# A decoder block on one core: loads and gathers moved across stage joins, row refills ahead of x, conditioning shared with TensorE

## The chip, the cores and the metric

The kernel runs on one core of one Trainium2 chip. The metric is the device time of one execution in microseconds (us); lower is better. The time before is the median of three runs. The profile is of one further execution, taken by the hardware profiler.

## The reference, cut to what matters

One layer of a decoder block over 2048 tokens of width 1024, all in float32. The conditioning vector c gives six vectors; a delta-rule head group and a dilated attention head group share one projection; a mixture of 32 experts follows.

```python
def reference(x, c, w_ada, b_ada, norm_mix, w_in, w_conv, ..., norm_final):
    for l in range(DEPTH):
        mod = c @ w_ada[l] + b_ada[l]                                  # 1024 x 6144
        sh_a, sc_a, gt_a, sh_f, sc_f, gt_f = jnp.split(mod[:, None, :], 6, axis=-1)
        h = rmsnorm(x, norm_mix[l]) * (1.0 + sc_a) + sh_a
        x = x + gt_a * hybrid_mixer(h, w_in[l], w_conv[l], ..., w_out[l], rel_bias[l])
        h = rmsnorm(x, norm_ffn[l]) * (1.0 + sc_f) + sh_f
        x = x + gt_f * hierarchical_moe(h, w_router_group[l], w_router_expert[l], w_gate[l], w_up[l], w_down[l])
    return rmsnorm(x, norm_final)

# hybrid_mixer: p = h @ w_in; first 1536 columns -> causal convolution of 4 taps, SiLU -> q, k, v of 4 heads
#   gated delta rule in chunks: a unit lower triangular solve per chunk, then a state carried over the chunks
#   attention of 8 heads in three dilated windows, merged by their log-sum-exp, rms norm
#   y = concat(delta rule part * silu(z), attention part) @ w_out
# hierarchical_moe: best of 4 groups, best 2 of its 8 experts, blocks of tokens per expert:
#   hid = silu(xb @ w_gate[e]) * (xb @ w_up[e]); ys = hid @ w_down[e]; out.at[tok].add(ys * gate)
```

## The kernel before, in words

`block_kernel` runs seven stages one after the other, with a barrier of all engines between them: `condition_and_project`, `project_channels`, `deltanet`, `attention`, `mix_and_route`, `experts`, `finish`. Each stage opens a `Room`, which takes its on-chip tiles and semaphores. Before the stage's work SyncE raises every semaphore of the stage that has a credit, one instruction each (L159); other engines enter the stage at once, but each wait includes the credit. At the end a room clears its semaphores and meets at the barrier (L138). The order of work on each engine is written out by hand in every stage; SyncE issues nearly all DMAs, strictly in program order, and stands at each `wait_ge` before them. Tokens are in 16 tiles of 128 (NT = 16, P = 128), D = 1024 = KD x 128.

**condition_and_project.** The six vectors are computed in 12 blocks of 512 columns (BANK), the first FIRST = 4 before all else, since they are shift and scale. The weights `w_ada` of a block come in two halves of 1 MB through NW = 3 buffers (`load_half`). VectorE multiplies each half's four slices with its scalars of c and adds them (`weigh`, L363 and L365: 4 instructions a half); then TensorE sums over the partitions with a matrix of ones (`over_partitions`, L285) and VectorE adds the bias (`take_mod`, L376). When all four are there, VectorE makes the gain (L399) and the first tiles of h, TensorE turns them (`turn`, L292) and multiplies with the token weights `wt` (L309), 4 MB in four DMAs, all of which it waits for. In the loop over the 16 tiles one more half per tile is weighed.

**project_channels.** TensorE computes 20 channels of 128 rows over 2048 tokens: 4 groups of 512 tokens each, 8 products a group (`group`, L644), weights `w_chan` of 0.5 MB a channel through two buffers (`load_w`, L509). ScalarE copies each group out of PSUM (`take_group`, L729); group n+2 waits for the copy of group n. At the start ScalarE computes decay values first (L759 to L763), after three small DMAs. The last channels run beside the solve of small 32 x 32 blocks on VectorE; SyncE stores the channels to DRAM (`store_cv`) and the solved blocks (`store_blocks`).

**deltanet.** A loop over 16 chunks. Per chunk SyncE loads `nt`, four pairs of small diagonal blocks into zeroed tiles `dz` and `dzt` (`load_solve`), `kc`, `vb`, `kg`, `qg`, `aqk` (`load_chain`), `z`, and, for the first eight chunks, 1 MB of q/k channels for the attention. TensorE's products (`heads`, L1050) and VectorE's masks and differences (L1164, L1170, L1174) alternate in one chain per chunk; L1136 is ScalarE's copy of a chunk's solution. VectorE begins with two operations on `nrm` (L1155, L1157) that need a square root of ScalarE. GpSimd zeroes `dz` and `dzt` at the start.

**mix_and_route** (the output stage). Per tile t and, in the code, its buffer b and count q: VectorE merges the three attention parts (`differences`, L1699 to L1701; `weigh`, L1705 to L1714; `normed`, L1718 and L1719), TensorE turns y (`turn_y`), multiplies with `w_out` (`out`, L1621, 32 records), turns h of an earlier tile (`turn_h`) and computes its router logits (L1615). VectorE adds the result to x (`add_out`, L1722 and L1723), normalizes (`router_in`, L1735 to L1737), and routes pairs of tiles (`choose` and `place` in alternate slots), whose lists GpSimd scatters to DRAM (L1581). In slot t VectorE does: `add_out(t-1)`, `weigh(t+2)`, `choose` or `place`, `router_in(t-1)`, `normed(t+2)`, `differences(t+3)`. TensorE in step t: `turn_y(t+1)`, `turn_h(t-2)`, `out(t)`, logits of t-2, ranks. ScalarE in slot t ends with the exponential of t+3 (L1886), then the logits copy (L1908), for which TensorE's next `turn_h` waits. SyncE's loop decides when rows come:

```python
with sp.Fori(0, NT // 2 - 2) as i:
    for b in range(2):
        load_x(2 * i + (2 + b), b, i + 1)     # waits for x2_out and h_ready of two tiles before
        load_y(2 * i + (4 + b), b, i + 2)     # waits for yt_done: y of two tiles before is turned
```

`load_y` loads 256 KB of y (L1545) and 792 KB of attention rows into `mo` (L1547). After the last x the stage loads the gate/up weights of the first NWB = 4 experts, 2 MB each, into `big`. After the last tile the places are computed on VectorE, GpSimd gathers the lists, and VectorE writes `slot_tok` (L1872) and `slot_gate` (L1873).

**experts.** Blocks of two half blocks of 64 rows. GpSimd gathers 128 rows of h by index (`gather`, L2060), TensorE turns them (L2094), ScalarE copies them (L2151), TensorE multiplies the upper half with `wgu` and the lower with a copy `wgu2` (L2108, L2109), which ScalarE makes (`copy_gate_up`, L2159); VectorE copies the w_down block (`copy_down`, L2195). At the start SyncE loads the four w_down blocks (L2030), 1 MB each, and only then reports them and the gate/up blocks as loaded.

## Time and profile before

| | |
|---|---|
| median of three runs | 2518.68 us (2518.53 to 2520.19) |
| the profiled execution | 2507.53 us, span 2505.4 us |
| mean granted TensorE clock | 0.949 |
| TensorE products | 2206.2 us busy (88% of the span) |
| VectorE | 1126.5 us (45%) |
| ScalarE | 922.0 us (37%) |
| GpSimd | 382.8 us (15%) |
| read from and written to memory | 296.84 and 124.85 MB |

A stage can be told by its lines: `condition_and_project` from 0 to 296 us, `project_channels` to 971, `deltanet` to about 1160, `attention` to 1515, `mix_and_route` to 1897, `experts` to about 2440, `finish` to the end. In the timeline one row is an instruction, or several alike on one engine merged (x8): start, duration, engine, line, operation, output<-inputs, shapes, and in brackets how long the engine had been idle before and what released it. A product in float32 leaves two records on TensorE. SPq rows are SyncE's issues of DMAs, not their transfers. The granted clock is 1.00 in the rows of a stretch that TensorE began cold, too; at 1.2 GHz a record of 512 columns takes about twice the time that it takes at 2.4 GHz.

### The profile page before, as it was taken

How to read it: one execution, taken by the hardware profiler on the slowest of the kernel's cores; microseconds unless marked ns; L12 is line 12 of the kernel's file. 1: busy time of each engine (PE TensorE's matmuls, PEld its weight loads, DVE VectorE, ACT ScalarE, POOL GpSimd, SP SyncE). 2: the span in 40 equal slices, each digit the busy share in tenths (PEclk: the TensorE clock that was granted, in tenths of full speed). 3: DMA queues.
4: the chain of work that ended last, by engine and by line, in shares of the span. 5: the costliest groups of instructions: out<-in, count | busy, mean ns of one | idle time of the engine just before them, and what ended most of it. 6: DMA issues, size and time to landing. Idle time of an engine off the chain costs nothing. (4 is left out here: it accounts for less than half of the span.)

```text
span 2505.4 us, 33260 instructions
## 1 busy us (share of the span) xinstructions
PE 2206.2 (88%) x9964; PEld 1242.9 (50%) x9965; DVE 1126.5 (45%) x2294; ACT 922.0 (37%) x2136; POOL 382.8 (15%) x320
## 2 busy tenths in 40 slices
PE   3999899999988897897999998878885998999990
PEld 2666544444444445896777774444552333333330
DVE  5444222232233752555888775656652222222223
ACT  1333111111233311224778774323323443444433
POOL 0000000000011101344333110010012222222220
PEclk9999999999999998998999999988887999999995
DMA  8444102211255544985223324343354988989747
GB/s 341 147 153 147 50 34 90 104 59 50 99 173 178 182 178 131 311 261 200 89 92 105 102 89 162 127 119 99 121 210 148 306 261 284 328 249 312 218 80 287
DMA packets 178320, 418.13 MB, mean 167 GB/s; under 512 B 41192, under 2 KB 81000, under 8 KB 162744
## 3 DMA queue, kind: packets, MB, share of 16 engines
q1 hardware_dynamic: 155944, 346.59, 39.6%
q0 software_dynamic: 13472, 45.26, 7.8%
q10 hardware_dynamic: 8816, 25.18, 2.9%
q8 instruction: 46, 0.75, 0.1%
q14 instruction: 42, 0.34, 0.0%
HBM read 296.84 MB, written 124.85 MB: 168 GB/s over the span
## 5 line engine op out<-in xcount | busy, mean ns | idle before, releaser
L644 PE MATMUL ps<-big,pc_w 128*128 128x512 f32 x1280 | 558.0, 597 | 10.6 <-DMA pc_w<-in_w_chan 10.6
L644 PEld LDWEIGHTS ps<-big,pc_w 128*128 128x128 f32 x1280 | 243.9, 192 | 312.3 <-issue 300.9
L2108 PE MATMUL ps<-big,ex_xt 128*64 x672 | 302.2, 603 | 2.1 <-ACT ex_xt L2151 2.1
L2109 PE MATMUL ps<-ex_wgu,ex_xt 128*64 128x512 f32 x672 | 302.2, 603 | 0.0
L1621 PE MATMUL ps<-w_out,mo_yt 128*128 128x512 f32 x512 | 235.5, 619 | 0.0
L309 PE MATMUL ps<-cp_wt,big 128*128 128x344 f32 x768 | 225.4, 454 | 0.0
L2159 ACT COPY ex_wgu<-big 128x4096 f32 x43 | 155.1, 3607 | 84.7 <-SPq L2025 51.9
L309 PEld LDWEIGHTS ps<-cp_wt,big 128*128 128x128 f32 x768 | 145.8, 191 | 76.9 <-issue 4.0
L1363 PE MATMUL ps<-at_v,at_pt 128*128 128x128 f32 (+1 forms) x1200 | 182.8, 290 | 0.0
L1429 ACT ACTIVATE at_p<-at_p,at_low 128x256 f32<-128x256 f32 (+1 forms) x384 | 174.0, 456 | 19.1 <-DVE at_low L1392 18.8
L2108 PEld LDWEIGHTS ps<-big,ex_xt 128*64 128x64 f32 x672 | 89.7, 139 | 181.1 <-issue 181.1
L1363 PEld LDWEIGHTS ps<-at_v,at_pt 128*128 128x128 f32 x1200 | 149.1, 191 | 46.1 <-issue 36.4
L1621 PEld LDWEIGHTS ps<-w_out,mo_yt 128*128 128x128 f32 x512 | 101.6, 202 | 121.3 <-issue 121.0
L2120 PE MATMUL ps<-ex_wd,ex_hidt 128*64 x336 | 153.2, 598 | 2.7 <-DVE mod L2185 1.5
L2121 PE MATMUL ps<-ex_wd,ex_hidt 128*64 128x512 f32 x336 | 153.2, 598 | 0.0
L1390 DVE SCALAR_TENSOR_TENSOR at_p<-ps,bias 128x512 f32<-128x512 f32 (+1 forms) x192 | 109.3, 569 | 68.0 <-PE ps L1338 67.9
L1338 PE MATMUL ps<-at_kb,at_qb 64*128 64x256 f32 (+1 forms) x768 | 119.1, 388 | 13.1 <-POOL at_kb L1324 12.1
L729 ACT COPY pc_pre<-ps 128x512 f32<-128x512 f32 x48 | 28.1, 586 | 277.9 <-PE ps L644 277.9
L804 DVE TENSOR_SCALAR pc_cv<-pc_pre,pc_wc 128x2048 f32<-128x2048 f32 x12 | 15.4, 1286 | 234.1 <-ACT pc_pre L729 234.1
L2204 DVE TENSOR_TENSOR ex_hid<-ex_sg,ps 128x256 f32<-128x256 f32 x42 | 17.7, 422 | 222.6 <-ACT ex_sg L2167 222.6
L2069 POOL DMA_INDIRECT acc_d<-mod,ex_to x42 | 85.5, 2035 | 209.0 <-DVE mod L2185 110.8
L1408 ACT COPY at_pt<-ps 128x512 f32<-128x512 f32 (+1 forms) x192 | 93.5, 487 | 58.6 <-PE ps L1348 53.3
(295 smaller groups left out, 3187.8 us busy)
## 6 DMA issues: line engine op xcount, KB each, us to landing
big<-in_w_gate_up SPq DMA_DIRECT2D x32, 2048.0 KB, 11.2
ex_wd<-in_w_down SPq DMA_DIRECT2D x32, 1024.0 KB, 6.6
cp_w<-in_w_ada SPq DMA_DIRECT2D x24, 1024.0 KB, 5.4
ch_d<-pc_cv SPq DMA_DIRECT2D x20, 1024.0 KB, 4.1
at_v<-v_d SPq DMA_DIRECT2D x27, 512.0 KB
o_d<-at_o SPq DMA_DIRECT2D x48, 264.0 KB, 2.1
mo<-o_d SPq DMA_DIRECT2D x16, 792.0 KB
pc_qkv<-ch_d SPq DMA_DIRECT2D x16, 768.0 KB, 5.6
```

The lines of the kernel that those rows point to most:

```text
L309: last = nc.tensor.matmul(ps[:, ROW_A + g, 0:THIRD], m.ht[:, k, t * P:(t + 1) * P], wt[:, k, g * THIRD:(g + 1) * THIRD], start=(k == 0), s ...
L644: last = nc.tensor.matmul(ps[:, n % 2, :], w[:, ch % 2, k, :], m.ht[:, k, g * BANK:(g + 1) * BANK], start=(k == 0), stop=(k == KD - 1))
L1338: last = nc.tensor.matmul(ps[:, 2 * (s % 2) + h, lo:2 * P], qb[r, b, s, :], kb[r, b, s, lo:], start=True, stop=True)
L1363: last = nc.tensor.matmul(ps[:, 6 + b, w], pt[:, e, h, k, :], v[:, b, k, w], start=(k == k0), stop=(k == 1))
L1390: nc.vector.scalar_tensor_tensor(p[:, s, :, lo:], ps[:, 2 * e:2 * e + 2, lo:2 * P], DH ** -0.5, bias[:, unit[0][1], 2 * s:2 * s + 2, lo:], ...
L1429: ins = nc.scalar.activation(p[:, s, h, lo:], p[:, s, h, lo:], ACT.Exp, bias=low[:, b, at:at + 1], accum_out=low[:, b, at + AH:at + AH + 1])
L1621: last = nc.tensor.matmul(ps[:, 2 + 2 * b + n, :], yt[:, b, k, :], w[:, k, n * BANK:(n + 1) * BANK], start=(k == 0), stop=(k == KD - 1))
L2108: nc.tensor.matmul(ps[0:HB, 2 + b, :], xt[:, b, k, 0:HB], wgu[:, bass.ds(at * WGU + k * 2 * DE, 2 * DE)], start=(k == 0), stop=(k == KD - 1))
L2109: last = nc.tensor.matmul(ps[HB:P, 2 + b, :], xt[:, b, k, HB:P], wgu2[:, b, k, :], start=(k == 0), stop=(k == KD - 1))
L2120: nc.tensor.matmul(ps[0:HB, 6 + c, :], hidt[:, b, k, 0:HB], wd[:, bass.ds(at * WD + (k * D + c * BANK), BANK)], start=(k == 0), stop=(k == ...
L2121: last = nc.tensor.matmul(ps[HB:P, 6 + c, :], hidt[:, b, k, HB:P], wd2[:, b, k, c * BANK:(c + 1) * BANK], start=(k == 0), stop=(k == DE // ...
L2159: nc.scalar.copy(wgu2[:, b, :, :].rearrange("p k n -> p (k n)"), wgu[:, bass.ds(at * WGU, WGU)]).then_inc(*wgu2_ready[b].inc)
```

## The change

It has eight parts. (1) In `mix_and_route` the y/`mo` refill is issued ahead of the x refill in SyncE's loop. (2) The weights of channel 0 get a tile of their own, `m.w_chan`, loaded in the middle of the first stage's loop; TensorE doesn't wait for them. (3) The first chunk's `nt`, `dz`, `dzt` and `kc` of the delta rule have their tiles in `m.mod` (`m.first`); GpSimd zeroes two of them at the start of `project_channels`, and SyncE loads them there between the stores of the last two channels. (4) Of the first four conditioning blocks VectorE weighs the first halves alone; the second halves are products of TensorE with `cb`, a copy of c spread over 128 columns, and `over_partitions` adds to them in PSUM. (5) The token weights are waited for in pairs. (6) w_down of the first four experts is loaded in the output stage, into the tile of `w_out`, after its last use. (7) GpSimd's gathers of the first two expert blocks are issued at the end of the output stage, straight by `slot_tok`. (8) In `experts` the first gate/up copy is VectorE's, ahead of the w_down copy. `bias` stays allocated and holds tiles of `experts`.

```diff
 # condition_and_project
+        cb = R.sb("cb", [P, KH, P])
+        pe_used, cb_ready = R.sig("pe_used"), R.sig("cb_ready")
+        chan_in = R.sig("chan_in", 16)
-        c_in, cst_in, wt_in, nrm_in = R.sig("c_in", 16), R.sig("cst_in", 16), R.sig("wt_in", 16), R.sig("nrm_in", 16)
+        c_in, cst_in, wt_in, nrm_in = R.sig("c_in", 16), R.sig("cst_in", 16), S("wt_in", KD // 2, 16), R.sig("nrm_in", 16)
...
                     if n >= NW:
-                        sp.wait_ge(*w_used.n(n - NW + 1))
+                        if on_pe(n - NW):
+                            sp.wait_ge(*pe_used.n((n - NW) // HALVES + 1))
+                        else:
+                            sp.wait_ge(*w_used.n(used_up_to(n - NW)))
...
                     store(t)
+                    if t == NT // 2:
+                        sp.dma_start(m.w_chan[:, :, :], a["w_chan"][0]).then_inc(*chan_in.inc)
+                sp.wait_ge(*chan_in.n(1))
...
-                    pe.wait_ge(*mod_ready.n(n))
-                    nc.tensor.matmul(ps[:, ROW_M, :], m.ones, acc[:, n % 2, :], start=True, stop=True).then_inc(*sum_done.inc)
+                    if n >= FIRST:
+                        pe.wait_ge(*mod_ready.n(n))
+                    nc.tensor.matmul(ps[:, row_m(n), :], m.ones, acc[:, n % 2, :], start=(n >= FIRST), stop=True).then_inc(*sum_done.inc)
+
+                def second_half(n):
+
+                    pe.wait_ge(*w_in[(HALVES * n + 1) % NW].n((HALVES * n + 1) // NW + 1))
+                    if n >= 2:
+                        pe.wait_ge(*mod_ready.n(n - 1))
+                    for k in range(KH):
+                        last = nc.tensor.matmul(ps[:, row_m(n), :], cb[:, k, :], w[:, (HALVES * n + 1) % NW, k, :], start=(k == 0), stop=False)
+                    last.then_inc(*pe_used.inc)
...
+                pe.wait_ge(*cb_ready.n(1))
+                second_half(0)
                 pe.wait_ge(*cst_in.n(1))
                 for n in range(FIRST):
+                    if n + 1 < FIRST:
+                        second_half(n + 1)
                     over_partitions(n)
...
+                V.tensor_copy(cb[:, :, :], ct[:, KH:].unsqueeze(2).to_broadcast([P, KH, P])).then_inc(*cb_ready.inc)
                 for blk in range(FIRST):
-                    for half in range(HALVES):
-                        weigh(HALVES * blk + half)
+                    weigh(HALVES * blk)
 # project_channels
-                load_w(0)
+                load_w(1)
                 sp.dma_start(al[:, :], row_bc(a["a_log"], GH)).then_inc(*small_in.inc)
                 sp.dma_start(dtb[:, :], row_bc(a["dt_bias"], GH)).then_inc(*small_in.inc)
                 sp.dma_start(wc[:, :], a["w_conv"]).then_inc(*small_in.inc)
-                load_w(1)
...
                 store_blocks(1)
                 store_cv(NCH - 2)
+                first_nt, dz, dzt, kc = m.first
+                sp.wait_ge(*blank.n(2))
+                sp.wait_ge(*nt_out[0].n(1))
+                sp.dma_start(first_nt, m.nt_d[0]).then_inc(*first_in.inc)
+                for k in range(P // SB):
+                    s = slice(k * SB, (k + 1) * SB)
+                    sp.dma_start(h4(dz[s, :])[:, :, s], small_blocks(m.xb_d, 0, k)).then_inc(*first_in.inc)
+                    sp.dma_start(h4(dzt[s, :])[:, :, s], small_blocks(m.xtb_d, 0, k)).then_inc(*first_in.inc)
+                sp.dma_start(h4(kc), m.ch_d[GH:2 * GH, :, 0:P].rearrange("c p n -> p c n")).then_inc(*first_in.inc)
                 store_cv(NCH - 1)
+                sp.wait_ge(*first_in.n(2 + 2 * (P // SB)))
...
+                for k in range(1, 3):
+                    nc.gpsimd.memset(m.first[k], 0.0).then_inc(*blank.inc)
...
-                    pe.wait_ge(*w_in[ch % 2].n(ch // 2 + 1))
+                    if ch:
+                        pe.wait_ge(*w_in[ch % 2].n((ch + 1) // 2))
 # deltanet
                 sp.dma_start(gain[:, :], row_bc(a["gdn_norm"], P)).then_inc(*gain_in.inc)
-                load_solve(0)
                 load_chain(0)
...
+                    if c:
+                        sp.dma_start(h4(kc[b][:, :]), m.ch_d[GH:2 * GH, :, c * P:(c + 1) * P].rearrange("c p n -> p c n")).then_inc(*k_in[b].inc)
 # mix_and_route
                     for b in range(2):
+                        load_y(2 * i + (4 + b), b, i + 2)
                         load_x(2 * i + (2 + b), b, i + 1)
-                        load_y(2 * i + (4 + b), b, i + 2)
...
+                sp.wait_ge(*w_done[1].n(PAIRS))
+                for e in range(NWB):
+                    sp.dma_start(m.wd[:, e * WD:(e + 1) * WD].rearrange("p (k n) -> p k n", k=DE // P), a["w_down"][e]).then_inc(*first_in.inc)
...
+                for b in range(2):
+                    pool.wait_ge(*h_out[b].n(NT // 2))
+                pool.wait_ge(*zero_out.n(2))
+                pool.wait_ge(*slots_ready.n(1))
+                for b in range(2):
+                    pool.indirect_dma_start(out=m.xg[:, b, :], out_offset=None, in_=m.h_d.rearrange("t p n -> (t p) n"),
+                                            in_offset=bass.IndirectOffsetOnAxis(ap=m.slot_tok[:, b:b + 1].bitcast(U32), axis=0)).then_inc(m.xg_in[b], 16)
 # experts
-                for b in range(NWB):
-                    load_down(b, b)
                 for b in range(NWB - 1):
-                    arrived(b, 0, 1)
+                    arrived(b, 0, 0)
...
-                gather(0, 0)
-                gather(1, 0)
...
-                copy_gate_up(0, 0)
                 take_x(0, 0, 0)
                 copy_gate_up(1, 1)
...
-                take_idx(0, 0)
-                take_idx(1, 1)
+                started = dve.value_load(m.by_block[0:1, 0, 0:1], min_val=1, max_val=NE)
+                at = dve.value_load(m.by_block[0:1, 2, 0:1], min_val=0, max_val=NWB - 1)
+                dve.wait_ge(*gu_loaded.n(started))
+                dve.sem_inc(seen_dve, 1)
+                nc.vector.tensor_copy(wgu2[:, 0, :, :].rearrange("p k n -> p (k n)"), wgu[:, bass.ds(at * WGU, WGU)]).then_inc(*wgu2_ready[0].inc)
                 copy_down(0, 0)
```

## Rows read from the trace of the kernel before

**Rows 1.** Windows: stretch, length, busy time (instructions) by engine, clock, DMA share, GB/s.

```profile
1554.90:1824.00 269.10, 229.38 (x791) 128.59 (x789) 162.24 (x430) 87.61 (x154) 22.24 (x20) 0.89 0.36 118
1824.00:1860.00 36.00, 35.27 (x135) 19.75 (x133) 21.41 (x70) 9.49 (x17) 5.36 (x4) 1.00 0.78 306
```

**Rows 2.** Waits, 1540 to 1960 us: total, times, longest.

```profile
DVE mo_lo L1699 <- DMA mo<-o_d: 93.3, 12, 11.2
```

**Rows 3.** Timeline of SyncE, the output stage.

```profile
1631.34 0.44 SPq L1547 DMA_DIRECT2D mo<-o_d  x1
```

**Rows 4.** Timeline of VectorE, the output stage.

```profile
1594.73 1.23 DVE L1722 TENSOR_TENSOR bias<-ps,mod 128x1024 f32<-128x1024 f32 x1
...
1609.18 0.75 DVE L1719 SCALAR_TENSOR_TENSOR mod<-mo,mo_ss,gain 128x512 f32<-128x512 f32 x1
...
1641.37 0.17 DVE L1699 TENSOR_TENSOR mo_lo<-mo 128x8 f32<-128x8 f32 x1 [10.49 <-DMA mo<-o_d]
```

**Rows 5.** Timeline of TensorE, the output stage.

```profile
1642.35 1.97 PE L1597 MATMUL ps<-cst,bias 128*128 128x128 f32 x8 [7.28 <-ACT lg L1908]
1644.11 15.26 PE L1621 MATMUL ps<-w_out,mo_yt 128*128 128x512 f32 x32
...
1806.29 14.39 PE L1621 MATMUL ps<-w_out,mo_yt 128*128 128x512 f32 x32
...
1824.00 13.90 PE L1621 MATMUL ps<-w_out,mo_yt 128*128 128x512 f32 x32
...
1841.36 7.03 PE L1621 MATMUL ps<-w_out,mo_yt 128*128 128x512 f32 x16
```

**Rows 6.** Timeline, the join to `project_channels`.

```profile
296.50 1.28 ACT L759 ACT_TABLE_LOAD   x1 [8.09 <-PEq L138]
...
303.92 30.15 PE L644 MATMUL ps<-big,pc_w 128*128 128x512 f32 x64 [10.56 <-DMA pc_w<-in_w_chan]
...
309.79 0.26 ACT L763 ACTIVATE pc_t<-pc_t 128x64 f32<-128x64 f32 x1
...
313.57 0.58 ACT L729 COPY pc_pre<-ps 128x512 f32<-128x512 f32 x1 [3.53 <-PE ps L644]
```

**Rows 7.** Timeline, the start of `deltanet` and two later chunks.

```profile
974.25 0.19 DVE L1157 TENSOR_SCALAR gd_nrm<-gd_nrm 128x64 f32<-128x64 f32 x1
...
978.60 0.50 SPq L977 DMA_DIRECT2D gd_vb<-vb_d  x1
...
979.41 2.04 PE L1050 MATMUL ps<-gd_dz,gd_nt 128*128 128x128 f32 x8 [15.53 <-DMA gd_dzt<-xtb_d]
...
981.49 0.69 DVE L1164 TENSOR_TENSOR gd_yy<-ps,cst 128x512 f32<-128x512 f32 x1 [7.04 <-PE ps L1050]
...
1010.42 0.58 ACT L1136 COPY gd_u<-ps 128x512 f32<-128x512 f32 x1 [2.69 <-PE ps L1050]
1026.10 0.58 ACT L1136 COPY gd_u<-ps 128x512 f32<-128x512 f32 x1 [9.04 <-PE ps L1050]
```

**Rows 8.** Timeline, the first four conditioning blocks.

```profile
14.93 2.07 PE L285 MATMUL ps<-cp_acc,cst 128*128 128x512 f32 x2 [14.93 <-DMA cst<-in_cst]
...
28.83 3.12 DVE L365 SCALAR_TENSOR_TENSOR cp_acc<-cp_w,cp_ct,cp_acc 128x512 f32<-128x512 f32 x4 [0.75 <-DMA cp_w<-in_w_ada]
...
41.90 0.69 DVE L376 TENSOR_TENSOR mod<-ps,cp_bb 128x512 f32<-128x512 f32 x1 [2.23 <-PE ps L285]
```

**Rows 9.** Timeline, the join to `experts`.

```profile
1893.88 0.29 DVE L1872 TENSOR_TENSOR slot_tok<-mo_fill,ps 128x128 int32<-128x128 f32 x1
...
1898.57 2.05 SPq L2030 DMA_DIRECT2D ex_wd<-in_w_down  x4
1898.76 0.94 POOL L2060 DMA_INDIRECT ex_xg<-h_d,ex_idx  x1 [7.70 <-DVE ex_idx L2188]
...
1907.78 1.97 PE L2094 MATMUL ps<-cst,ex_xg 128*128 128x128 f32 x8 [14.40 <-DMA ex_xg<-h_d,ex_idx]
...
1911.00 1.11 PE L2108 MATMUL ps<-big,ex_xt 128*64 x1 [1.25 <-ACT ex_xt L2151]
```

123 lines of the change are left out of this document (68 added, 55 removed).

## The prediction

> **What bounds the kernel now.** TensorE is busy most of the span, so a change pays either where TensorE stands still or where it runs at the lower clock. I looked for such places in the view by windows, then in the waits, then in the timeline around each place the diff touches. In the steady part of the output stage (tile 2 to tile 14) TensorE is busy 229.4 of 269.1 us, at a granted clock of 0.89, while in the 36 us after it both are full [rows 1]. The wait list names the cause: VectorE waits 93.3 us in 12 waits for the attention rows (`mo`) [rows 2]. The timeline shows how it spreads. SyncE issues the refill of `mo` for tile t+3 at 1631.34, right behind the refill of x, and it lands 10.0 us later, when VectorE starts again at 1641.37 after 10.49 us of idleness [rows 3, 4]. ScalarE's exponential stands behind that, the logits copy stands behind the exponential on ScalarE, and TensorE waits 7.28 us for that copy; after it the transposes take 1.97 and the 32 records of the output projection 15.26 us, against 13.90 us when nothing stopped the engine (1824.00) [rows 5]. So each late refill is paid twice, once as waiting and once as the lower clock. The other places are joins: 10.6 us of TensorE before the first channel product [rows 6], 15.5 us before the delta-rule stage [rows 7], and the stretch from the last routing result at 1894.17 to the first expert product at 1911.00 [rows 9].
>
> **1. Output stage: row refills ahead of x.** Today a refill of y/`mo` stands on SyncE behind the refill of x, which waits for `h_ready`, the last VectorE work of the slot; right after it VectorE wants the rows. Swapped, the refill for t+3 waits only for the transpose of y of t+1, which TensorE does within some 3 us after the end of the last projection. VectorE comes to the rows 15.2 us after it starts the slot (1594.73 to 1609.93) [rows 4], so some 12 us are left for a landing that took 6.5 to 11.2 us. Covered, then: its cover is VectorE's own slot. What is late next? VectorE's slot of 15.2 + 0.6 us against TensorE's step. Two steps without a refill in them show the latter: 1806.29 to 1824.00 and 1824.00 to 1841.36, 17.71 and 17.36 us [rows 5], mean 17.54. So TensorE is next, VectorE has 1.7 us to spare. From 1554.88 to 1824.00 lie 12 steps: 269.1 - 12 x 17.54 = 58.6 us; I take **58** for small waits that the clean steps don't show. x itself is refilled one issue later in order, but it still waits for `h_ready` and is needed two slots on, some 20 us after; nothing.
>
> **2. First channel weights a stage ahead.** The join costs 303.92 - 296.50: ScalarE and VectorE enter the stage at 296.5, SyncE first raises its semaphores, and the weights land at 303.92 [rows 6]. With the weights there, TensorE enters with the others at 296.6: **7.3 us**. What is next is ScalarE, which copies the first group at 313.57 but is through with its own start at 310.05 [rows 6]; the first group now ends at 306 and the third needs that copy only at 313, so it is covered. The 0.5 MB load moves into the middle of the projection loop, where one load more on SyncE holds nobody up; free.
>
> **3. First chunk of the delta rule.** The ten DMAs (nt, eight small blocks, kc) move behind the store of the last channel but one, on a SyncE queue that then only waits for the last channel; free. In the new stage TensorE starts at once, but VectorE reaches the first mask only after its scale factors, at 974.44 instead of 981.49 [rows 7]: at most 7.0 us. SyncE issues vb of the first chunk at 973.9 instead of 978.60, so everything behind it moves by 4.7 us only, and the second chunk's blocks are wanted right away. Later the stage is held by loads (ScalarE has the third chunk's result at 1010.42 after 2.69 us of waiting, the fourth's 15.68 us later after 9.04 [rows 7]), which could give back part: bounds 2 and 7, I take **4.7**, the shift of the queue.
>
> **4. Conditioning shared.** VectorE loses four halves of 3.1 us; TensorE gets four groups of 4 products with 512 columns (8 records). A product of this shape, two records, took 2.07 us at the lower clock [rows 8]. A restart costs some 2.5 us: the first channel group, 16 records, took 9.65 us with the hand-over of 0.2 [rows 6], and half of the 13.90 us of 32 records is 6.95. A group is thus 3.5 us at the full, 6 to 7 at the lower clock. The stretch is bound by arrival: VectorE waits for half 5 until 28.83 [rows 8], and at 2.5 us a half (1 MB at the 420 GB/s of that time) half 3 lands near 21.3 and the last near 34. Followed through: the first group of TensorE from 11 to 17, the next from 21.6 to 28; the refill into that buffer is now issued at 28 instead of 25, so the last half lands near 36; the group then ends at 40 to 43, the last gain is ready at 42.4 to 45.3 instead of 42.6 (41.90 + 0.69) [rows 8]. At the full clock throughout it would be 40. The six more semaphores delay the first DMA by 0.3 us (contained). Bounds: 2.5 gained, 3 lost; I take **0.5 lost**.
>
> **5. Join to the experts.** GpSimd's two gathers now follow `slot_tok` at 1894.17 [rows 9]: 0.94 + 0.3 + 0.94 us, so the stage ends 2.1 us later, and the next has its semaphores up at 1900.7, 2.1 us after 1898.57, where SyncE's first DMA went out [rows 9]. Before, the first gather started at 1898.76 and the transposes at 1907.78 [rows 9], 9.0 us later, with 4 MB of w_down on the same engines; now those 4 MB go under the routing tail from about 1858 on (stated on the old clock), where DMA has room. Started at 1894.3, the gather lands at 1903.3 at the latest, at the earliest it is not what is waited for; plus 1.97 and 1.0 us for transposes and copy, the first expert product starts between 1904 and 1906.5 instead of 1911.00 [rows 9]. VectorE's copy of the gate/up block (twice the 1.23 us of a w_down block) ends by 1903.4; covered. I take **5.5**, range 4.5 to 7. The Trainium skill, "DMA: Bandwidth & Descriptors", section "Anatomy of one DMA — SWDGE (gpsimd) path", puts such a DMA at about 2.0 us plus its bytes at 436 GB/s, an estimate of 3.2 us here; by that the gain would be 7 and the sum 1.5 us lower; the row, with its contention, says 9.0, and no row shows the gather alone.
>
> **Sum:** -58 - 7.3 - 4.7 + 0.5 - 5.5 = -75.0 us. Nothing else bounds these stretches in common, as all stages are joined by barriers. The profiled execution has a span of 2505.4 and a time of 2507.5 us; changed, 2430.4 and 2432.5. The runs' median stands 11.2 us above it, and I carry that along: 2518.7 - 75 = **2443.7 us**.
>
> **Rivals.**
> A. The clock stays low in the output stage. If short waits in every step were enough to bring the lower clock back, 11 of the steps would each keep 15.4 - 13.9 and 1.97 - 1.04 us, together 2.4: 26 us, a time of 2470. Against it: 1824.00 ran in 13.90, and the step behind it in 17.36 with a short wait in it [rows 5]. The Trainium skill, "TensorE: Matmul & The Clock Gate", section "A second HAM failure mode: psum-queue depth-cycling", describes just this, frequent small stops between groups that cycle through PSUM banks; the trace here agrees only for the stops of 2 us and more. 0.09.
> B. The refill is hidden in part. If 4 of 7.8 us stay, VectorE's slot is 19.8 us and takes TensorE's place: 12 x 2.3 = 27 us, 2471. For it: landings of 10 to 11 us where scatters run beside them. 0.08.
> C. The swap does nothing, because SyncE gets to the refill no sooner (another wait of its queue comes last): only the joins remain, 17 us, 2502. 0.05.
> D. Slower: x, now behind the rows, arrives late and is what VectorE's addition waits for. It decides only once x lands over 20 us after `h_ready`; to eat the joins too, the slots must grow from 22.4 to over 23.8 us. At 25 us it gives 12 x 2.6 - 17 = +14, 2533. Landings of x of about 5 us speak against it. 0.02.
> E. More than forecast (conditioning all at the full clock, chunk 1 not late, gather early): -84, 2435. 0.08. The forecast itself with its terms' bounds, 2436 to 2456: 0.68.
>
> **How the numbers follow.** Likeliest 2443.7. Forecast and E together hold 0.76 between 2433 and 2456; to pass 0.8 the range takes in the lighter cases of A and B, up to 2466. A measurement tells about 0.2%, 5 us, from no change. Slower: 0.02. Within 5 us of no change: 0.02, C with a loss at the start. Faster: 0.96.
>
> **What the changed profile would show.** VectorE's waits for `mo` in the output stage fall from 93 to under 10 us; start to start of the 32-record projections is 17.4 to 17.9 us and each takes 13.90. The wait before the first channel product is 4 us instead of 11.4; before the delta-rule stage TensorE stands 7 us, but VectorE's first mask is at 3.6 us from the stage's start. The x norm gain after conditioning is ready between 40 and 45 us. First expert product 10 us after the last `slot_tok` instead of 17. I would be wrong above all if the projections still start 20 us or more apart: then the wait before them names the engine that took the refill's place.

## The result, and the profile after

The changed kernel took 2440.9 us (median of 4 runs, 2435.7 to 2443.9) against 2518.6 us, a ratio of 0.969 with a 95% interval of 0.9675 to 0.971. The forecast was 2443.7. Three executions of the runs below, of 4.6 to 11.1 ms, lie far outside all other times of their kernels and stand in no median or range. The profiled execution of the changed kernel took 2443.9 us with a span of 2441.8, so between the two profiled executions lie 63.6 us and between the medians 77.7. The experiments have to say which of the two the terms of the forecast should be held against.

The head of the page of the changed kernel:

```profile
span 2441.8 us, 33277 instructions
PE 2204.0 (90%) x9996; PEld 1242.2 (51%) x9997; DVE 1117.0 (46%) x2278; ACT 918.4 (38%) x2135; POOL 384.8 (16%) x320
PEclk8999999999999999999999999999978999999995
```

First the place of the largest term, the output stage. The windows of the changed kernel (columns as in [rows 1]), over the same twelve steps that [rows 1] shows in 269.1 us:

```profile
1551.90:1761.00 209.10, 209.10 (x790) 117.21 (x790) 158.27 (x423) 85.99 (x152) 22.31 (x20) 1.00 0.47 147
```

TensorE is busy in all of it (209.10 of 209.10 us), at the full clock (2.4 GHz). [rows 1] has 39.7 us of standing in its 269.1, so of the 60.0 us that are gone 39.7 were waiting and 20.3 were products that took longer at the lower clock. The waits of the stage, 1540 to 1900 us, where [rows 2] has 93.3 us of VectorE for `mo`:

```profile
DVE bias L1782 <- PE ps L1681: 48.8, 15, 7.0
```

No wait for `mo` is in the list any more; VectorE now waits for TensorE's projection, which is slack. The timeline of one step shows the order that was swapped (SyncE, then VectorE and TensorE; compare [rows 3 to 5]):

```profile
1568.80 0.34 SPq L1595 DMA_DIRECT2D mod<-y_d  x1
1569.33 0.39 SPq L1597 DMA_DIRECT2D mo<-o_d  x1
1576.87 0.34 SPq L1603 DMA_DIRECT2D bias<-in_x  x1
...
1583.25 1.23 DVE L1782 TENSOR_TENSOR bias<-ps,mod 128x1024 f32<-128x1024 f32 x1 [5.83 <-PE ps L1681]
...
1585.65 0.18 DVE L1765 TENSOR_TENSOR mo_ws<-mo_wt,mo 128x24 f32<-128x24 f32 x1
...
1569.31 13.90 PE L1681 MATMUL ps<-w_out,mo_yt 128*128 128x512 f32 x32
1586.53 13.90 PE L1681 MATMUL ps<-w_out,mo_yt 128*128 128x512 f32 x32
```

The rows are requested at 1569.33, 7.5 us ahead of x, and VectorE never stands in front of them. Step to step are 17.2 us here, 17.42 in the mean of twelve.

The conditioning, where TensorE now has half of the products (TensorE, then VectorE; compare [rows 8]):

```profile
11.33 6.14 PE L315 MATMUL ps<-cp_w,cp_cb 128*128 128x512 f32 x8 [11.33 <-DMA cp_w<-in_w_ada]
21.70 6.07 PE L315 MATMUL ps<-cp_w,cp_cb 128*128 128x512 f32 x8 [4.23 <-DMA cp_w<-in_w_ada]
29.50 3.67 PE L315 MATMUL ps<-cp_w,cp_cb 128*128 128x512 f32 x8 [0.88 <-DVE mod L412]
37.53 6.70 PE L315 MATMUL ps<-cp_w,cp_cb 128*128 128x512 f32 x8 [3.50 <-DMA cp_w<-in_w_ada]
...
45.99 0.69 DVE L412 TENSOR_TENSOR mod<-ps,cp_bb 128x512 f32<-128x512 f32 x1 [0.17 <-PE ps L307]
46.72 1.23 DVE L435 SCALAR_TENSOR_TENSOR mod<-mod,cp_nrm 128x1024 f32<-128x1024 f32 x1
```

The last group waits for its half until 37.53 and takes 6.70 us, nearly all at the lower clock (8 records of 512 columns take 3.5 us at the full one), and the x norm gain starts to be formed at 46.72 instead of 42.62. The join behind it in the changed kernel, and then the windows over the first 9.7 us of channel products, of the kernel before and of the changed one:

```profile
300.77 1.28 ACT L808 ACT_TABLE_LOAD   x1 [8.12 <-PEq L139]
300.81 15.69 PE L693 MATMUL ps<-big,w_chan 128*128 128x512 f32 x36 [3.22 <-PEq L139]
```

```profile
303.90:313.60 9.70, 9.68 (x17) 4.28 (x18) 0.67 (x3) 3.83 (x8) 2.03 (x2) 0.75 0.25 73
```

```profile
300.80:310.50 9.70, 9.69 (x23) 4.44 (x24) 0.32 (x3) 2.39 (x3) 0.95 (x2) 1.00 0.26 79
```

TensorE starts with ScalarE, after 3.22 us of standing instead of 10.56 [rows 6]. In this profile it also starts at a granted clock of 1.00 where it had a mean of 0.75: 23 records instead of 17 in the same time.

The delta-rule stage, from its entry to the first chunk's result (compare [rows 7]):

```profile
964.16 1.28 ACT L1174 ACT_TABLE_LOAD   x1 [5.51 <-PEq L139]
964.19 2.05 PE L1099 MATMUL ps<-mod 128*128 128x128 f32 x8 [6.17 <-PEq L139]
967.19 0.43 SPq L1028 DMA_DIRECT2D gd_vb<-vb_d  x1
967.69 0.68 DVE L1214 TENSOR_TENSOR gd_yy<-ps,cst 128x512 f32<-128x512 f32 x1
977.25 1.13 PE L1099 MATMUL ps<-gd_dz,gd_nt 128*128 128x128 f32 x8 [2.23 <-issue]
979.37 0.59 ACT L1186 COPY gd_u<-ps 128x512 f32<-128x512 f32 x1 [13.51 <-PE ps L1099]
```

The first mask is formed 3.5 us and the first result 15.2 us after the entry; before, they took 10.7 and 21.1 us (970.83 to 981.49 and 991.91). So the mask comes 7.1 us earlier and the result 5.9. In between TensorE, which takes its products in program order, stood 2.23 us before a product on the second chunk's blocks (`gd_dz`, 977.25). The join to the experts (compare [rows 9]):

```profile
1831.15 0.29 DVE L1932 TENSOR_TENSOR slot_tok<-mo_fill,ps 128x128 int32<-128x128 f32 x1
1832.27 0.94 POOL L1650 DMA_INDIRECT bias<-h_d,slot_tok  x1 [3.97 <-DVE slot_tok L1932]
1833.52 0.94 POOL L1650 DMA_INDIRECT bias<-h_d,slot_tok  x1 [0.30 <-issue]
1841.74 0.91 DVE L2233 MEMSET mod<- 128x1024 f32 x1 [10.10 <-PEq L139]
1842.64 1.94 PE L2149 MATMUL ps<-cst,bias 128*128 128x128 f32 x8 [11.98 <-SPq L160]
1846.40 1.11 PE L2163 MATMUL ps<-big,bias 128*64 x1 [1.82 <-DVE ex_wgu L2255]
```

Here the picture is not the forecast one. The gathers are issued early, but the next stage is not entered until 1841.74, 10.6 us after the last `slot_tok` instruction started, where before it took 3.0 us. Of the 5.5 us that I took (7 at best), 1.9 are left. TensorE no longer waits for the gather here: the turned rows are ready at 1845.6 and the first product waits some 0.6 us more for VectorE's copy of the gate/up block (L2255).

### The profile page after: what moved, and what is told of

Its sections match the earlier page's. It is cut to its first block and busy times, and to the rows that moved or that the text cites. A ratio compares the mean times of both kernels' runs of the same rounds, so it can differ in the third digit from the quotient of the medians.

```text
span 2441.8 us, 33277 instructions
## 1 busy us (share of the span) xinstructions
PE 2204.0 (90%) x9996; PEld 1242.2 (51%) x9997; DVE 1117.0 (46%) x2278; ACT 918.4 (38%) x2135; POOL 384.8 (16%) x320
## 5 line engine op out<-in xcount | busy, mean ns | idle before, releaser
L2163 PE MATMUL ps<-big,bias 128*64 x672 | 301.4, 602 | 2.7 <-DVE ex_wgu L2255 1.8
L2164 PE MATMUL ps<-ex_wgu,bias 128*64 128x512 f32 x672 | 301.4, 602 | 0.0
L693 PE MATMUL ps<-big,w_chan 128*128 128x512 f32 x640 | 279.9, 597 | 3.2 <-PEq L139 3.2
L693 PE MATMUL ps<-big,pc_w 128*128 128x512 f32 x640 | 278.2, 593 | 0.0
L1681 PE MATMUL ps<-w_out,mo_yt 128*128 128x512 f32 x512 | 223.7, 594 | 0.0
L693 PEld LDWEIGHTS ps<-big,w_chan 128*128 128x128 f32 x640 | 121.9, 192 | 154.4 <-issue 154.4
L693 PEld LDWEIGHTS ps<-big,pc_w 128*128 128x128 f32 x640 | 121.2, 191 | 149.3 <-issue 149.3
L2163 PEld LDWEIGHTS ps<-big,bias 128*64 128x64 f32 x672 | 89.6, 138 | 181.0 <-issue 181.0
L2175 PE MATMUL ps<-w_out,bias 128*64 x336 | 153.2, 598 | 2.6 <-DVE mod L2239 1.5
L2176 PE MATMUL ps<-ex_wd,bias 128*64 128x512 f32 x336 | 153.2, 598 | 0.0
L853 DVE TENSOR_SCALAR pc_cv<-pc_pre,pc_wc 128x2048 f32<-128x2048 f32 x12 | 15.4, 1286 | 225.3 <-ACT pc_pre L778 225.3
```

The costliest lines, as they stand in the source:

```text
L693: last = nc.tensor.matmul(ps[:, n % 2, :], w[ch % 2][:, k, :], m.ht[:, k, g * BANK:(g + 1) * BANK], start=(k == 0), stop=(k == KD - 1))
L1681: last = nc.tensor.matmul(ps[:, 2 + 2 * b + n, :], yt[:, b, k, :], w[:, k, n * BANK:(n + 1) * BANK], start=(k == 0), stop=(k == KD - 1))
L2163: nc.tensor.matmul(ps[0:HB, 2 + b, :], xt[:, b, k, 0:HB], wgu[:, bass.ds(at * WGU + k * 2 * DE, 2 * DE)], start=(k == 0), stop=(k == KD - 1))
L2164: last = nc.tensor.matmul(ps[HB:P, 2 + b, :], xt[:, b, k, HB:P], wgu2[:, b, k, :], start=(k == 0), stop=(k == KD - 1))
L2175: nc.tensor.matmul(ps[0:HB, 6 + c, :], hidt[:, b, k, 0:HB], wd[:, bass.ds(at * WD + (k * D + c * BANK), BANK)], start=(k == 0), stop=(k == ...
L2176: last = nc.tensor.matmul(ps[HB:P, 6 + c, :], hidt[:, b, k, HB:P], wd2[:, b, k, c * BANK:(c + 1) * BANK], start=(k == 0), stop=(k == DE // ...
```

## The experiments

All ran on one core each, and each ratio is against executions of the kernel before that were taken beside it (medians 2512.5 to 2514.5 us). In the table each figure is the distance of two times in the profiled execution of that kernel, start to start where nothing else is said. "Gain" is the start of the instruction that forms the x norm gain; "join 1" from there to the first channel product; "channels" from there to the end of the last channel product; "delta" from ScalarE's first activation in the delta-rule stage to the last chunk's result, with "first" the part up to the first result; "output" from the first transpose of the output stage to the last `slot_tok`; "join 2" from there to the first expert product; "in" the part of it up to VectorE's first instruction in the experts stage.

```
kernel          gain  join 1 channels first   delta  output join 2 (in)    span
before          42.62 261.30 659.96   19.79  176.39  378.56 17.12  (2.99)  2505.4
b_again         42.92 261.95 660.16   19.91  177.28  377.30 17.04  (2.99)  2506.7
b_swap          42.88 261.56 659.91   19.76  178.78  318.53 17.04  (2.99)  2451.8
b_wchan         42.08 254.02 656.60   18.48  181.67  382.93 17.27  (2.99)  2504.5
after           46.72 254.09 657.21   13.92  178.08  319.39 15.25  (10.59) 2441.8
a_again         46.54 255.13 657.78   13.91  175.42  317.37 15.08  (10.42) 2435.8
a_noswap        44.01 255.10 654.59   14.00  172.49  382.55 15.27  (10.61) 2493.9
a_cond_dve      43.55 254.25 657.43   13.10  172.02  318.57 15.03  (10.36) 2431.1
a_nochunk       43.21 253.79 656.98   21.03  183.02  319.15 15.35  (10.68) 2439.0
a_qk2           44.74 255.08 657.82   13.02  179.15  319.05 15.02  (10.36) 2438.6
a_qk_end        45.64 254.11 659.41   13.07  162.95  317.16 15.00  (10.34) 2434.7
a_gather_back   44.10 255.11 657.77   13.90  171.13  318.51 12.72  (4.76)  2429.8
a_late          44.76 255.03 657.84   13.84  171.93  319.18 11.18  (2.99)  2431.2
a_best          43.55 254.54 657.72   12.98  172.04  318.24 11.15  (2.99)  2428.0
```

### Both kernels again (b_again, a_again)

> The kernel before, unchanged, profiled a second time, to see how far a stage moves from one execution to the next. Its first profiled execution took 2507.5 us, the median of its runs is 2518.6. Theory: the difference sits in stretches that are paced by loads (the delta-rule stage, the output stage), which change from execution to execution; the delta-rule stage, 177.7 us from its entry at 970.8 to the last chunk's result at 1148.5 in the first profile, is then up to 5 us longer or shorter here, and the twelve output steps (269.1 us) by up to 8 us, while the conditioning (x norm gain at 42.6 us) and the channel products agree within 0.5 us. Rival: all stages scale alike; then the time from the start to 964 us differs too, by some 4 us.

> The changed kernel, unchanged, profiled a second time. Its first profiled execution stands 63.6 us in span below that of the kernel before, its median 77.7 us below. Theory: the output steps, no longer held by refills, repeat within 0.5 us (12 steps from 1551.89 to 1760.97, 209.1 us), and what moves is the delta-rule stage (179.4 us from entry to last result). Time 2436 to 2444 us. Rival: the first comparison of the two profiles is off by chance in the conditioning too: then the x norm gain is ready near 43 us instead of 46.7.

The kernel before: median 2512.5 us over 13 runs beside these, from 2506.9 to 2521.4, and as `b_again` 2515.8 over seven, from 2508.9 to 2517.1. Its second profiled execution took 2508.9 us, the lowest of those seven. The changed kernel: 2435.3 us (2432.2 to 2437.9), ratio 0.9686 [0.966, 0.971]. The two pairs of profiles differ by 63.6 and by 70.9 us in span. From one execution of the same kernel to the next the output stage of the kernel before moved by 1.3 us, the delta-rule stage by 1 to 3 us, the twelve output steps of the changed kernel by nothing I can see (34.9 us for each pair of steps in both). That is less than I expected of the kernel before: no profile shows one of its longer executions. In the other two profiles with the old order of refills the output stage took 382.6 and 382.9 us instead of 377 to 379, so a scatter of about 5 us does sit there. Against the medians the profiled pairs show too small a gain: both profiles of the kernel before come from its low end, and both of the changed kernel are the longest of their four executions (2443.9 and 2437.9 us).

### The swap alone, and all but the swap (b_swap, a_noswap)

```diff
                     for b in range(2):
-                        load_x(2 * i + (2 + b), b, i + 1)
                         load_y(2 * i + (4 + b), b, i + 2)
+                        load_x(2 * i + (2 + b), b, i + 1)
```

> The kernel before with one edit: in the loop of the output stage the refill of the attention rows is issued ahead of the refill of x. Theory: this edit alone takes 58 to 60 us, so the time is 2459 to 2462 us; the 32-record projections start 17.4 us apart. Rival: the edit needs the other parts beside it (the loads of the joins), or gains what they gain too: a time over 2470 or under 2450.

> The changed kernel with that one edit undone. Theory: the joins are worth what the two profiles show outside the output steps, 63.6 - 60.0 = 3.6 us, and up to 17 us by the forecast; so 2501 us by the forecast of the joins, 2510 to 2515 us by the profiles. The twelve steps take about 269 us again.

The swap alone: 2448.9 us (2443.9 to 2454.0) against 2512.5, ratio 0.974 [0.971, 0.976], 63.6 us. All but the swap: 2494.2 us, ratio 0.992 [0.990, 0.995], 18.3 us. Windows of `b_swap` over its twelve steps, then the wait for `mo` in `a_noswap` between 1540 and 1900 us:

```profile
1560.80:1770.20 209.40, 209.40 (x789) 117.27 (x789) 158.41 (x426) 86.02 (x152) 22.30 (x20) 1.00 0.47 147
```

```profile
DVE mo_lo L1759 <- DMA mo<-o_d: 95.6, 12, 11.9
```

The swap gives full steps without any other part, and without the swap the wait is back at 95.6 us. The first expectation gave 58 to 60 us from its profile; the output stage of the profile moved by 59 (377.9 in the mean to 318.5), the runs by 63.6. The second expectation from the profiles (2510 to 2515) missed; the forecast's (2501) was nearer, and still 7 us too long. The first pair of profiles understates what lies outside the output stage: 4.4 us of its 63.6, against 11.0 of the 70.9 in the second pair and 15.5 between `before` and `a_noswap`. 63.6 + 18.3 is 81.9, with 77 for both together; the difference is within what the intervals allow. Taken last, beside the other parts, the swap is worth 58.9 us (2494.2 - 2435.3).

### The first channel weights alone (b_wchan)

```diff
                     store(t)
+                    if t == NT // 2:
+                        sp.dma_start(m.w_chan[:, :, :], a["w_chan"][0]).then_inc(*chan_in.inc)
...
-                load_w(0)
+                load_w(1)
```

> The kernel before with one edit: the first channel weights are loaded in the middle of the token projection. Theory: two gains, not one. The wait goes (7.0 us from the x norm gain to the first channel product, 261.6 against 254.6 us), and TensorE, standing 3 us instead of 10.6, stays at the full clock, so the first group of 16 records takes 7.0 us instead of 9.65: 2.6 us more. Time 9.6 us under the kernel before. Rival (the forecast): 7.3 us, the clock falls all the same; then the stretch from the first to the last channel product is 660 us as before and not 657.4.

Measured: 2505.6 us against 2514.5, ratio 0.9966 [0.995, 0.998], 8.9 us by the medians. The interval spans 5 to 12 us and so holds both the theory's 9.6 and the rival's 7.3; only the profile can tell them apart. TensorE in its join:

```profile
296.10 8.39 PE L648 MATMUL ps<-big,w_chan 128*128 128x512 f32 x19 [3.18 <-PEq L138]
```

19 records in 8.39 us, full clock from the first one. Join 1 fell from 261.6 (mean of three) to 254.0, the channel products from 660.0 to 656.6, and the time by 8.9 us. That looks like the theory's two gains, the wait and the lower clock behind it. The other ten profiles with the weights ahead show that the second is not to be counted on. They all have the same stop of 3.2 us before the first product, but this is the window over the first ten microseconds of channel products in `b_wchan`, in `a_late` and in `a_best`:

```profile
296.10:306.10 10.00, 10.00 (x24) 4.50 (x25) 0.32 (x3) 2.76 (x3) 0.00 (x0) 1.00 0.28 75
```

```profile
299.79:309.79 10.00, 10.00 (x20) 4.53 (x21) 0.32 (x3) 2.99 (x4) 0.95 (x2) 0.84 0.27 76
```

```profile
298.09:308.09 10.00, 10.00 (x17) 4.25 (x18) 0.32 (x3) 2.43 (x3) 0.94 (x2) 0.70 0.28 75
```

24 records, 20, or 17, against 18 in each of three profiles with the stop of 10.6 us. At 0.43 us a record (the full clock, 13.90 us for 32) that is 2.6 us gained, 0.9 gained or 0.4 lost; three profiles show 24, five 20 and three 17, in the mean 1.0 us. The stretch is 2.6 us shorter on average because the clock also fell less in a second place, 370 to 420 us behind the first product, where TensorE stands 4.8 to 6.7 us in every kernel. The windows there, of the kernel before and of `a_late`:

```profile
673.92:723.92 50.00, 44.34 (x143) 24.27 (x142) 17.44 (x55) 15.09 (x64) 6.80 (x6) 0.93 0.33 97
```

```profile
669.79:719.79 50.00, 43.35 (x157) 24.49 (x156) 20.00 (x63) 16.75 (x70) 7.70 (x7) 1.00 0.40 122
```

The granted clock is 0.93 in each of the three old profiles, and 0.93 in three, 0.97 in five and 1.00 in three of the eleven with the weights ahead. By ScalarE's copies of the groups that place brings 2.1 us in the mean, and 0.4 of it goes again between 450 and 560 us. Whether the edit has anything to do with that second place I can't say: `b_wchan` itself has 0.93 there.

### The sharing undone (a_cond_dve)

```diff
         def on_pe(n):
-            return n < HALVES * FIRST and n % HALVES == 1
+            return False
...
                 for blk in range(FIRST):
-                    weigh(HALVES * blk)
+                    for half in range(HALVES):
+                        weigh(HALVES * blk + half)
```

> The changed kernel with the sharing of the conditioning undone: VectorE weighs all eight halves again, the split of the wait for the token weights stays. Theory: the sharing cost time, because its products ran at the lower clock and the last group waited for the last half: the x norm gain is ready at 42.5 to 43.5 us instead of 46.7, and the kernel is 3 to 4 us faster than the changed one. Rival (the forecast): the sharing costs 0.5 us, then there is no difference to be seen. A third: it gains, because VectorE's halves would have ended later without it; then the kernel is slower.

Measured: 2436.9 us, ratio 0.970 [0.969, 0.971], no difference from the changed kernel's 0.969. The gain starts at 43.55 us. That it was 46.7 with the sharing is true of two profiles only; over all eight with it the time runs from 43.21 to 46.72 with a mean of 45.0. What decides is the last group of TensorE, behind whose end the gain comes 2.5 us later. Here it is in `a_nochunk`, where the gain comes at 43.21:

```profile
37.03 3.70 PE L315 MATMUL ps<-cp_w,cp_cb 128*128 128x512 f32 x8 [2.66 <-DMA cp_w<-in_w_ada]
```

It takes 3.70 us here, 5.2 to 5.4 in five profiles and 6.7 in two, as the clock was granted, and it begins between 36.2 and 38.7 us, as the half arrives. So the theory's mechanism is right and its size is that of two profiles: the sharing costs 1.4 us on average, and this cannot be seen in the times.

### The first chunk's loads back in their stage (a_nochunk)

```diff
                 store_cv(NCH - 2)
-                sp.dma_start(first_nt, m.nt_d[0]).then_inc(*first_in.inc)
...
                 sp.dma_start(gain[:, :], row_bc(a["gdn_norm"], P)).then_inc(*gain_in.inc)
+                sp.dma_start(first_nt, m.nt_d[0]).then_inc(*first_in.inc)
...
                 load_chain(0)
```

The one line stands for all ten loads.

> The changed kernel with the ten loads of the first delta-rule chunk back at the start of their stage. Theory: the first chunk's result is there 5 to 7 us later after the stage's entry (15.2 us in the changed kernel, 21.1 in the one before), but the last result is not, within 2 us, because the chunks in between are paced by the DMA engines: no difference in time to be seen. Rival (the forecast): the kernel is 4.7 us slower than the changed one.

Measured: 2444.0 us (2441.2 to 2450.1), ratio 0.973 [0.972, 0.975], that is 3.1 us over the changed kernel's first median and 8.7 over its second. My theory, that all is given back, fell. It rested on one pair of profiles, 176.4 us without and 178.1 with the early loads. Over all profiles in which only this part of the stage differs, the five without it have 176.4, 177.3, 178.8, 181.7 and 183.0 (mean 179.4), the seven with it 178.1, 175.4, 172.5, 172.0, 171.1, 171.9 and 172.0 (mean 173.3): 6.1 us, as much as the first result came earlier (19.8 and 13.7 us in the mean).

### The q and k loads beside the chunks (a_qk2, a_qk_end)

```diff
-                    if c < m.NCH - NCONV:
-                        sp.dma_start(m.qk[:, c, :], m.ch_d[NCONV + c]).then_inc(*later_in.inc)
+                    if c % 2 == 0 and c // 2 < m.NCH - NCONV:
+                        sp.dma_start(m.qk[:, c // 2, :], m.ch_d[NCONV + c // 2]).then_inc(*later_in.inc)
```

> The changed kernel with the eight 1 MB loads of the attention stage's q and k rows, which run beside chunks 1 to 8 of the delta-rule stage, issued beside every second chunk instead. Theory: the chunks are paced by the DMA engines while those loads run (share of 0.95 to 1.1 where chunks take 10 to 17 us, against 9.33 us a chunk afterwards). With half the extra bytes per chunk most chunks take 9.3 to 10 us: the stage, 164.2 us from the first to the last result against 15 x 9.33 = 140, is 12 to 22 us shorter, the kernel 2420 to 2430 us. Rival: the chunks wait for the order of the queue and for buffers, not for bytes; then the stage is as long as before, and the late loads of q and k delay the attention stage.

Measured: 2441.4 us, ratio 0.971 [0.970, 0.973], no gain. Chunks 2 to 16 took 166.1 us: those beside a load 11.5 to 14.1 us, late in the stage too. The theory of a limit on bytes within a chunk fell; the rival's second half did not hold either, the attention stage began as early after the last result as before.

```diff
+                    if c == NT - 3:
+                        for j in range(m.NCH - NCONV):
+                            sp.dma_start(m.qk[:, j, :], m.ch_d[NCONV + j]).then_inc(*later_in.inc)
```

> The changed kernel with the eight loads of q and k rows (1 MB each) issued together behind the last chunk's loads instead of beside chunks 1 to 8. Spreading them over twice as many chunks moved nothing: each cost a chunk about 3 us wherever it stood. Theory: they delay the chunk loads that are issued behind them on the same queue; with nothing behind them they delay nothing, all chunks take 9.3 to 9.6 us, and from the first to the last result 140 to 146 us pass instead of 157 to 166; the eight loads take 20 to 25 us, of which some 18 lie beside the last two chunks. Time 10 to 18 us under the changed kernel. Rival: the chunk loads themselves hold the stage; then it is not shorter by more than 3 us, and the end of the loads is added to it.

Measured: 2435.7 us, ratio 0.968 [0.967, 0.969], no gain over the changed kernel's 0.9686. With nothing beside them the fifteen chunks took 149.9 us instead of 157 to 166, and the next stage began 28.3 us after the last result instead of 14.8. SyncE at the end of the stage:

```profile
1119.54 4.74 SPq L1065 DMA_DIRECT2D big<-ch_d  x8
...
1130.59 21.35 SPq L1046 DMA_DIRECT2D y_d<-gd_o  x2
```

What the chunks won, 7 to 14 us, the end paid with 13.5: the last stores of results stand on SyncE's queue behind the eight loads, and ScalarE waits 15.7 us for one of them. The eight loads cost about the same wherever they go. Even without them ten of the 149.9 us are stalls against 9.33 us a chunk, most of it in two chunks of 12.8 and 13.5 us; what these wait for the profile doesn't name. Which limit of the DMA side this is, these two runs don't settle.

### The gathers back in the experts stage (a_gather_back, a_late)

```diff
-                for b in range(2):
-                    pool.indirect_dma_start(out=m.xg[:, b, :], out_offset=None, in_=m.h_d.rearrange("t p n -> (t p) n"),
...
+                for b in range(2):
+                    pool.indirect_dma_start(out=m.xg[:, b, :], out_offset=None, in_=m.h_d.rearrange("t p n -> (t p) n"),
                 pool.wait_ge(*zero_set.n(1))
```

> The changed kernel with the two gathers of the first expert block back at the start of the experts stage; the loads of w_down stay early. Theory: an issued gather holds the end of the stage until it has landed. The experts stage is then entered 2.4 us after the last routing result, as in the kernel before, instead of 10.3 us, the gathers are issued some 2 us later and land after 5 to 6 us, since no w_down load runs beside them; first expert product 14 to 16 us after that result, against 15.2 in the changed kernel and 17.1 in the one before: the early issue is worth nothing, or less. Rival (the forecast): the early issue is worth 4 to 5 us, and the first product comes 19 us or more after the result.

Measured: 2432.4 us, ratio 0.969 [0.967, 0.970]. In the profile the first expert product comes 12.7 us after `slot_tok`, against 15.0 to 15.4 with the early gathers:

```profile
1820.55 0.29 DVE L1929 TENSOR_TENSOR slot_tok<-mo_fill,ps 128x128 int32<-128x128 f32 x1
1825.31 0.91 DVE L2233 MEMSET mod<- 128x1024 f32 x1 [4.27 <-PEq L139]
1825.73 0.94 POOL L2127 DMA_INDIRECT bias<-h_d,slot_tok  x1 [7.95 <-POOLq L139]
1830.05 1.97 PE L2149 MATMUL ps<-cst,bias 128*128 128x128 f32 x8 [9.99 <-DMA bias<-h_d,slot_tok]
```

The first gather is there 4.3 us after it is issued, and by the profile the early issue costs 2.3 us or more. The entry takes 4.8 us though, not 3.0. In this kernel GpSimd still waited for `slot_tok` at the end of the routing stage, with nothing to do after it. The next run takes that wait away, with the three for earlier stores that stand ahead of it:

```diff
-                pool.wait_ge(*slots_ready.n(1))
```

> The changed kernel with the two gathers at the start of the experts stage again, as in the run before this one, and with GpSimd's wait for the last routing result (and for the stores of h) gone from the end of the routing stage. Theory: with that wait GpSimd is the last engine to leave the stage and 1.8 us of its own way out are seen; without it the experts stage is entered 3.0 us after the start of the last slot_tok instruction, as in the kernel before, instead of 4.8, and the first expert product starts 11.0 us after it, against 12.7 with the gathers late and 15.1 with them early; 4 us less than the changed kernel. Rival: the 1.8 us come from the early loads of w_down; then nothing moves against the run before (12.7 us).

```profile
1823.29 0.29 DVE L1925 TENSOR_TENSOR slot_tok<-mo_fill,ps 128x128 int32<-128x128 f32 x1
1826.28 0.91 DVE L2229 MEMSET mod<- 128x1024 f32 x1 [2.50 <-PEq L139]
1827.94 2.69 POOL L2123 DMA_INDIRECT bias<-h_d,slot_tok  x1 [0.30 <-issue]
1828.22 2.29 DVE L2251 COPY ex_wgu<-big 128x4096 f32 x1 [1.03 <-SPq L2077]
1834.47 0.18 PEld L2159 LDWEIGHTS ps<-big,bias 128*64 128x64 f32 x1 [1.65 <-issue]
```

Entry after 2.99 us, first product after 11.2: both as expected. The loads of w_down are early in this kernel too, so they were not the cause. Time 2433.8 us, ratio 0.968 [0.966, 0.969]; 4 us are 0.16% and the intervals overlap, so the profile shows this gain and the times allow it.

What holds the end of the stage is in an instruction that the timeline leaves out: the DRAIN of GpSimd, its last step in a stage's block before it meets the others at the barrier. By line, with the duration in ns and the start in us, in the kernel before, the changed kernel, `a_gather_back` and `a_late`:

```profile
L1540 POOLq DRAIN  x1: 2831/2831/2831, 1892.7 to 1892.7; - x1
```

```profile
L1590 POOLq DRAIN  x1: 7843/7843/7843, 1832.5 to 1832.5; - x1
```

```profile
L1590 POOLq DRAIN  x1: 2834/2834/2834, 1821.1 to 1821.1; - x1
```

```profile
L1590 POOLq DRAIN  x1: 2831/2831/2831, 1822.1 to 1822.1; - x1
```

In all fourteen profiles VectorE's first instruction of the next stage starts 1.35 to 1.37 us after this DRAIN ends. It takes 2.83 us in the seven kernels that issue no gather there, and 7.6 to 7.9 us in the seven that do. There it ends 1.8 to 1.9 us after the last bytes of the gathers, while these land 7.1 to 7.5 us after the last `slot_tok` instruction began: it moves with the landing. The 1.8 us between the entries of `a_gather_back` and `a_late` are explained too. Without the waits the DRAIN starts 1.2 us before the last `slot_tok` instruction and runs beside it; with them it starts 0.6 us after.

### Both losing parts undone (a_best)

> The changed kernel with its two losing parts undone: the conditioning on VectorE alone, and the gathers at the start of the experts stage with no wait on GpSimd ahead of them. Theory: x norm gain at 42.6 to 43.6 us (1 to 3 us less than in the changed kernel's profiles), first expert product 11.0 us after the last slot_tok instruction instead of 15.1, so 5 to 7 us under the changed kernel: ratio to the kernel before 0.966 against 0.969. Rival: both differences are at the edge of what a profile repeats, and the ratio is 0.968 to 0.970 as before.

Measured: 2430.2 us (2425.6 to 2435.4), ratio 0.968 [0.966, 0.970]; span 2428.0, the shortest of all. Gain at 43.55 us and first product 11.15 us after `slot_tok` came as expected. The runs don't tell the ratio from 0.969, so by the times this was the rival's outcome; the version is at least as fast as the changed kernel.

## Why the prediction was right

The predicted time, 2443.7, lies 3 us from the measured one. The terms one by one:

**Output steps, -58.** 269.1 us became 209.1, 60.0, with 17.42 us a step where I took 17.54 from two clean steps [rows 5]. "Paid twice" holds: 39.7 us of waiting and 20.3 of the lower clock. The cover held: VectorE's slot absorbed every landing, what is next is TensorE, at the full clock. The 6.5 to 11.2 us that I called landings are VectorE's waits; from issue to use the old kernel took 6.1 to 10.7 us, and the new order leaves 7.5 to 11.8. Rival A (the clock stays low) did not come, the window reads 1.00; its condition, a short wait in every step, did not come either, so these runs don't test it. Nor did B or C, there is no wait for `mo`; nor D, none for x. By the runs the swap alone is worth 63.6 us, and 58.9 when it is taken last.

**Channel weights, -7.3.** Join 1 is 7.0 us shorter over all profiles, and the wait before the first product is 3.2 us. What I had not in the sum is the clock. I noted that the first group took 9.65 us after a stop of 10.6 and used that for the conditioning, but didn't ask here what the clock does after a stop of 3.2. The answer is 0.4 us lost to 2.6 gained, 1.0 in the mean of eleven profiles, and 1.6 us more from later places in the stretch whose tie to the edit is open. `b_wchan` measured 8.9 for the edit alone.

**First chunk, -4.7.** Over twelve profiles 6.1 us, within the bounds of 2 to 7. The first comparison seemed to say that all was given back (178.1 against 176.4), which was scatter of this stage, 171 to 178 us for the same code. The expected giving back did not happen: what the first chunk gained stayed. I took the shift of SyncE's queue for the whole gain; it was 4.7 us as read (`vb` is issued 3.0 us after the entry instead of 7.8), but the first result came 6.1 us earlier in the mean, between that and the 7.1 us of the mask.

**Conditioning, +0.5.** +2.3 us over all profiles (45.0 against 42.6), within the bounds of -2.5 and +3. 0.9 of it is there without the sharing. The chain I followed, last half at 36 and last group of 3.5 or 6 to 7 us, gave 42.4 to 45.3; over eight profiles the group begins at 36.2 to 38.7, 37.0 in the mean, and takes 3.7 to 6.7.

**Experts, -5.5.** This failed: -1.9, outside 4.5 to 7. The step at fault is "so the stage ends 2.1 us later". It counted GpSimd's issue of the two gathers and nothing after it; the stage ended 7.5 us later. The view of the DMA engines from 1832 to 1842 us of the changed kernel, in 40 slices of 0.25 us, shows the traffic of the two gathers over at about 1838.5:

```profile
GB/s 0 0 0 0 0 0 0 115 33 98 147 295 393 442 377 311 311 279 360 311 279 115 115 115 82 16 0 0 0 0 0 0 0 0 0 0 0 0 0 0
```

GpSimd's DRAIN ends 1.9 us after that, at 1840.4, and the next stage begins at 1841.74. `a_gather_back` and `a_late` show that with the gathers in the next stage the DRAIN is back at 2.83 us and the entry is early again. The other half of the term was off as well, in the other direction: without w_down beside it a gather landed in 4.3 us instead of the 9.0 of [rows 9]. The 3.2 us that I worked out from the Trainium skill, "DMA: Bandwidth & Descriptors", section "Anatomy of one DMA — SWDGE (gpsimd) path", are nearer to that measurement than my row.

**Sum.** The spans of the two pairs of profiles differ by 67 us in the mean: gain +3.9, join 1 -7.0, channels -2.6, output -59.6, join 2 -1.9, and -0.1 for the delta stage in those four profiles. The forecast had -75.0, and the medians show -77.7 and -77.2. The largest part of the distance is that the profiled executions of the kernel before were short ones: I carried 11.2 us from the profile to the median on both sides, and in the changed kernel the distance was -3.0. Errors of both signs then met: the channel stretch (2.6), the first chunk (1.4) and the output steps (2 to 6) for more gain, the experts' join (3.6) and the conditioning (1.8) for less. The total was better than its terms, and that it came within 3 us is luck.

**The signs.** No wait for `mo`, projections of 13.90 us that start 17.2 to 17.7 us apart (17.4 to 17.9 forecast) and a first mask at 3.5 us (3.6) came. The stop before the first channel product is 3.2 us where I wrote 4, and it was 10.56 before [rows 6], not the 11.4 that I wrote beside it. Two signs failed: the x norm gain came at 46.7 us in the first profile, outside 40 to 45, and the first expert product 15.3 us after the last `slot_tok` instead of 10. That 10 was the best case; my 5.5 us mean 11.6.

## What to carry to other kernels

Order the refills of a queue by who wants them first and by what each waits for: here one swap of two lines held nearly all of the gain, because a late refill was paid as a wait and again as the lower clock. Starting a transfer ahead of a stage's end only helps if the end doesn't have to outlast it: a DMA issued by GpSimd as the last thing of a stage cost more than it brought, because GpSimd's DRAIN stood until it had landed, while loads that landed long before the end were free. Even a wait without work, last on GpSimd, put 1.8 us of its DRAIN in sight. And don't read a difference of a few microseconds in a DMA-paced stage from one profile of each kernel: the same code moved by 7.
